# Feed-forward layers of a ten-layer fp32 network in two halves, with high and low input parts in one 512-column product

## What is computed

```python
def rmsnorm(x, g):
    return x * rsqrt(mean(x * x, -1) + eps) * g
def modulate(x, g, c_act, w, b):
    m = c_act @ w + b
    shift, scale, gate = jnp.split(m, 3, axis=-1)
    h = rmsnorm(x, g) * (1.0 + scale[:, None, :]) + shift[:, None, :]
    return h, gate[:, None, :]
def swiglu(h, w_gate, w_up, w_down):
    return (jax.nn.silu(h @ w_gate) * (h @ w_up)) @ w_down
# four times (ffn0 to ffn3):  x = x + 0.5 * g * swiglu(h, ...)
# twice (cffn0, cffn1): h = rmsnorm(x, g); a, b = split(h @ w_up);
#   x = x + (silu(causal_dwconv(a, w3, b3)) * b) @ w_down       (3 taps)
```

## Time and profile before

| | |
|---|---|
| median of 3 runs (lowest, highest) | 1868.75 us (1866.80, 1869.99) |
| span of the profiled execution, first to last instruction | 1865.1 us |
| TensorE busy, matmul / weight load | 1803.1 us / 1733.4 us, 14574 each |
| DVE / ACT / POOL busy | 1323.5 / 948.5 / 377.5 us |
| TensorE clock granted, mean | 0.994 of full |
| read from HBM | 368.89 MB, 198 GB/s over the span |

### The profile page before, as it was taken

One profiled execution on the slowest core, in us unless ns is written; L12 is line 12 of the kernel. 1 busy time (PEld: TensorE's weight loads), 2 busy tenths in 40 slices (PEclk: granted clock), 3 DMA queues, 4 the chain that ended last, 5 costly groups with the idle time before them and its releaser, 6 DMA issues.

```text
span 1865.1 us, 36260 instructions
## 1 busy us (share of the span) xinstructions
PE 1803.1 (97%) x14574; PEld 1733.4 (93%) x14574; DVE 1323.5 (71%) x1824; ACT 948.5 (51%) x1357; POOL 377.5 (20%) x371
## 2 busy tenths in 40 slices
PE   3999999999999999999999999999999999999998
PEld 2999989979999999999889999988999989689998
DVE  6677877888767576768876555897666767866665
ACT  3554555474645465446465445316544533764453
POOL 1222200051222122211143221002222200431221
PEclk9999999999999999999999999999999999999999
DMA  9877835745577647675924554313555533134551
GB/s 376 319 274 279 324 113 181 277 151 226 184 290 264 256 179 293 253 279 177 372 92 161 188 191 180 142 62 114 177 183 180 180 143 133 41 109 167 191 187 67
DMA packets 51059, 371.10 MB, mean 199 GB/s; under 512 B 5664, under 2 KB 5664, under 8 KB 6048
## 3 DMA queue, kind: packets, MB, share of 16 engines
q1 hardware_dynamic: 41760, 302.85, 44.4%
q0 software_dynamic: 9216, 67.11, 9.2%
HBM read 368.89 MB, written 1.05 MB: 198 GB/s over the span
## 4 chain that ended last, share of the span: by engine, by line
PE 83%; DVE 10%; ACT 4%; issue 1%; DMA 1%; POOL 0%; POOLq 0%; SPq 0%; DVEq 0%; ACTq 0%
PE gu L721 39%; PE acc L729 8%; PE acc L728 8%; PE acc L730 8%; DVE arena L2424 3%; PE gu L1054 2%; PE gu L1193 2%; PE gu L728 2%; PE gu L730 2%; PE gu L729 2%; DVE w_lo L1876 2%; DMA mring<-in_mods 1%; DVE mring L1891 1%; DVE arena L2166 1%; PE acc L1264 1%
## 5 line engine op out<-in xcount | busy, mean ns | idle before, releaser
L1876 DVE TENSOR_TENSOR w_lo<-ring,w_hi 128x2048 fp32r<-128x2048 f32 x265 | 613.7, 2319 | 271.6 <-ACT w_hi L1442 271.5
L1442 ACT ACTIVATE w_hi<-ring 128x2048 fp32r<-128x2048 f32 x265 | 504.9, 1907 | 74.6 <-PE acc L730 49.3
L721 PE MATMUL gu<-Hs_hi,w_hi 128*128 128x258 f32 (+1 forms) x2112 | 427.8, 284 | 2.5 <-DVE Hs_lo L1940 1.3
L721 PE MATMUL gu<-Hs_lo,w_hi 128*128 128x258 f32 (+1 forms) x2112 | 423.1, 282 | 0.0
L721 PE MATMUL gu<-Hs_hi,w_lo 128*128 128x258 f32 (+1 forms) x2112 | 422.5, 281 | 0.0
L651 POOL TENSOR_TENSOR arena<-arena,rstd 128x512 f32<-128x512 f32 x132 | 201.0, 1523 | 831.1 <-ACT arena L1456 778.4
L721 PEld LDWEIGHTS gu<-Hs_hi,w_hi 128*128 128x128 f32 x2112 | 325.7, 189 | 4.8 <-issue 1.8
L721 PEld LDWEIGHTS gu<-Hs_hi,w_lo 128*128 128x128 f32 x2112 | 325.8, 189 | 0.0
L721 PEld LDWEIGHTS gu<-Hs_lo,w_hi 128*128 128x128 f32 x2112 | 325.4, 189 | 0.0
L729 PE MATMUL acc<-hid_lo,w_hi 128*128 128x256 f32 x1056 | 297.8, 282 | 0.0
L728 PE MATMUL acc<-hid_hi,w_hi 128*128 128x256 f32 x1056 | 296.4, 281 | 1.2 <-DVE hid_lo L2095 1.2
(11 more groups left out here) (413 smaller groups left out, 2841.5 us busy)
## 6 DMA issues: line engine op xcount, KB each, us to landing
ring<-in_weights SPq DMA_DIRECT2D x276, 1024.0 KB, 4.8
mring<-in_mods POOLq DMA_DIRECT2D x64, 1024.0 KB, 6.1
mring<-in_mods SPq DMA_DIRECT2D x8, 1024.0 KB, 7.5
con<-in_constants SPq DMA_DIRECT2D x1, 1408.0 KB, 12.1
X<-in_x SPq DMA_DIRECT2D x1, 1024.0 KB, 7.2
out<-X SPq DMA_DIRECT2D x1, 1024.0 KB, 3.9
cact<-in_c SPq DMA_DIRECT2D x1, 512.0 KB, 3.3
vec<-in_vectors SPq DMA_DIRECT2D x1, 498.0 KB, 4.1
```

What stands on the lines that cost most here:

```text
L721: ins = mm(dst, part, x_lo if i == 1 else x_hi, start=start and i == 0, stop=stop and i == 2, skip_group_check=True)
L1442: act.activation(w_hi[buffer_of(n0, s)][:, :], ring[:, n % RING, :], ACT.Copy).then_inc(hi_ready, 1)
L1876: dve.tensor_tensor(w_lo[b][:, :], ring[:, n % RING, :], w_hi[b][:, :].bitcast(F32), ALU.subtract).then_inc(split_ready, 1)
```

## The change

What it does, on each engine:

- **The order of a layer.** 12 gate/up slots, 6 down slots (hidden tiles 0 to 11), 10 gate/up slots, 5 down slots (hidden tiles 12 to 21). Down goes output tile by output tile, over all hidden tiles of the half, with the last two hidden tiles of outputs 0 to 2 put behind their others; each output tile has a bank of `acc` for itself (m % 4), and each half is added to X by itself (`partial`). `clear` is gone. All is written out, without hardware loops. The weights are packed on the host in the new order; slots and bytes are as many as before.
- **Three bare hidden tiles.** Hidden tiles 0, 1, 2 are computed from the bare input as before (`bare_gate_up`, 258 columns in the layers with a shift; tile 2 in two banks of `acc`). Meanwhile the input is normalised in place, tile by tile: DVE multiplies X by gain and `row` (`scaled`), ACT adds the shift and rounds to `Hs_hi` (`normal`), DVE subtracts (`normal_low`). From hidden tile 3 on the input is final, and no shift columns and no scaling by POOL are needed.
- **The 512-column product.** For hidden tiles 3 to 21 and for all of down a product is two matmuls (`paired`): `w_hi` by the high and the low input side by side (512 columns, read from two places, `twin`) into the two halves of a bank, and `w_lo` by the high input (256 columns) onto the first half. The two halves are added behind PSUM: gate/up by ACT, which copies the second halves out (`low_half`), and DVE, which adds the first halves (`add`); down by two DVE operations into X.
- **Work that moves.** The multiplication by up and the low part of the hidden tile go from DVE to POOL (`mul`, `low`); the first of the three taps goes to ACT (`tap`). DVE's `low` for a slot now comes two slots ahead instead of three, behind `add`.
- The tiles of the next layer are entered one by one as the second half finishes them. The modulation loads keep their order by number; their folds lie at the slots of `FOLD_SLOTS`.

The diff, cut to its core:

```diff
+HALF_F0, HALF_N = (0, 12), (12, 10)
+DOWN_SLOT, DOWN_N = (12, 28), (6, 5)
+def down_tiles(half):
+    n = HALF_N[half]
+    order = [(m, f) for m in range(3) for f in range(n - 2)]
+    order += [(m, f) for m in range(3) for f in (n - 2, n - 1)]
+    return order + [(m, f) for m in range(3, KD) for f in range(n)]
...
# TensorE
+            def paired(bank, w, cols, x_both, x_hi, start, stop):
+                mm(bank.rearrange("p (a t) -> p a t", a=2), w_hi[w][:, cols], x_both, start=start, stop=False,
+                   skip_group_check=True)
+                return mm(bank[:, 0:L], w_lo[w][:, cols], x_hi, start=False, stop=stop, skip_group_check=True)
+                def gate_up(f):
+                    s = gu_slot(f)
+                    pe.wait_ge(split_ready, s0 + s + 1)
+                    pe.wait_ge(pair_free, f0 + (f - 2 if f < BARE_F + 2 else f - 1))
+                    bank = bank_of(f)
+                    for k in range(KD):
+                        if f == BARE_F:
+                            state["nh"] += 1
+                            pe.wait_ge(nh_ready, state["nh"])
+                        for e, cols in enumerate(columns(k)):
+                            ins = paired(bank[:, e, :], buffer_of(n0, s), cols, hs_twin(k), Hs_hi[:, k, 0:L],
+                                         start=(k == 0), stop=(k == KD - 1))
-                def clear():
-                    for b in range(4):
-                        mm(acc[:, b, :], zeros[:, 0:P], zeros[:, 0:1].to_broadcast([P, 512]), start=True, stop=True,
-                           skip_group_check=True)
...
-                gate_up(1)
-                clear()
-                with pe.Fori(0, ROUNDS) as it:
-                    for s in (2, 5):
-                        gate_up(s, it)
-                        gate_up(s + 1, it)
-                        down(s + 2, (s - 2) // 3, it)
-                down(FSLOTS - 1, PAIRS - 1, last=True)
+                bare_gate_up(1)
+                bare_gate_up(2)
+                for f in range(BARE_F, HALF_F0[1]):
+                    gate_up(f)
+                down(0)
+                for f in range(HALF_F0[1], NF):
+                    gate_up(f)
+                down(1)
...
# ScalarE, the start of a layer with a shift
+                high(n0, 2)
+                root(D, acc[:, 3, :])
+                evacuate(0)
+                high(n0, 3)
+                act.wait_ge(spread_ready, state["spread"])
+                act.activation(row, acc[:, 3, L:2 * L], ACT.Copy).then_inc(row_ready, 1)
+                silu(0)
+                evacuate(1)
+                for m in range(3):
+                    normal(m)
+                high(n0, 4)
+                for m in range(3, KD):
+                    normal(m)
+                silu(1)
+                high(n0, 5)
+                evacuate(2)
+                high_hidden(0)
+                high_hidden(1)
+                silu(2)
+                high_hidden(2)
...
+                    low_half(f)
+                        high_hidden(f - 1)
+                        high(n0, s + 3)
+                        silu(f)
# VectorE
+                low(n0, 3)
+                dve.wait_ge(row_ready, i + 1)
+                scaled(0)
+                scaled(1)
+                for m in range(KD):
+                    normal_low(m)
+                    if m + 2 < KD:
+                        scaled(m + 2)
+                low(n0, 4)
...
+                        add(f)
+                        low(n0, s + 2)
...
+                    fold_at(s)
+            def partial(m, how):
+                bank = acc[:, m % 4, :]
+                    link(dve.scalar_tensor_tensor(out=X[:, m, :], in0=bank[:, L:2 * L], scalar=gate[:, how, m:m + 1],
+                                                  in1=X[:, m, :], op0=ALU.mult, op1=ALU.add))
+                    return dve.scalar_tensor_tensor(out=X[:, m, :], in0=bank[:, 0:L], scalar=gate[:, how, m:m + 1],
+                                                    in1=X[:, m, :], op0=ALU.mult, op1=ALU.add)
# GpSimd, the start of a layer
+                scale(0)
+                scale(1)
+                mul(0)
+                mul(1)
+                scale(2)
+                low(0)
+                low(1)
+                mul(2)
+                low(2)
```

More of the change, by code:

```diff
@@ L655, in ffn @@
                         done += 1
-                assert done == len(folded)
+                    mul(f)
+                    low(f)
+                assert done == len(folds)
             ffn("ffn0")
@@ L678, in _ @@
         def _(pe):
-            state = dict(h=0, free=0, sq=0, misc=0, split=0, hid=0, rcp=0, presum=0, conv=0)
+            state = dict(h=0, nh=0, free=0, sq=0, misc=0, split=0, hid=0, rcp=0, presum=0, conv=0)
             mm = pe.matmul
@@ L1386, in norm @@
             def norm(scale, shift=None, mod=False, dest=H, parts=False, hi=None):
-                for m in range(KD):
-                    state["x"] += 1
-                    act.wait_ge(x_ready, state["x"])
-                    act.activation(H[:, m, :], X[:, m, :], ACT.Square).then_inc(sq_ready, 1)
                 root(D)
@@ new lines, in ffn @@
+                if conv:
+                    tap(0)
+                    tap(1)
+                    high(n0, 5)
+                    silu(0)
+                    silu(1)
+                    evacuate(2)
+                    high_hidden(0)
+                    high_hidden(1)
+                    low_half(3)
+                    tap(2)
+                    high(n0, 6)
+                    tap(3)
+                    silu(2)
+                    high_hidden(2)
+                else:
+                    silu(1)
+                    high(n0, 5)
+                    evacuate(2)
+                    high_hidden(0)
+                    high_hidden(1)
+                    silu(2)
+                    high_hidden(2)
@@ new lines, in ffn @@
+                for s in range(DOWN_SLOT[1], FSLOTS):
+                    if s == DOWN_SLOT[1]:
+                        if conv:
+                            silu(NF - 1)
+                        high_hidden(NF - 1)
+                    if s + 3 < FSLOTS:
+                        high(n0, s + 3)
+                    elif then is not None and s + 3 < FSLOTS + 2:
+                        if s + 3 == FSLOTS and extra is not None:
+                            extra()
+                        high(then, s + 3 - FSLOTS)
+                    if tiles is not None:
+                        for m in finished_in(1, s):
+                            tiles(m)
@@ L2112, in ffn @@
                 state["hid"] += NF
-                state["split"] += FSLOTS
-                update_ffn(n0, how, then, square=i != 1, enter=enter, scale=scale, parts=parts)
             def misc_wait():
```

671 lines of the change are left out of this document (401 added, 270 removed).

## The result

| | before | after |
|---|---|---|
| median of 5 runs each, in turns (lowest, highest) | 1866.80 us (1865.88, 1869.99) | 1874.58 us (1872.01, 1876.22) |
| ratio, 95% interval | | 1.0041 (1.0028 to 1.0053) |
| span of the profiled execution | 1865.1 us | 1873.6 us |

A forecast was written before the change was run, and what follows sets the result against it. TensorE's matmuls were taken as the bound, busy 1803.1 of 1865.1 us. 1865.1 - 31.1 (products) - 5.3 (`clear`) - 2 (layer ends) + 14 (layer starts) = 1840.7 us span, so 1844 median; range 1809 to 1869.

The forecast's parts named there:

- Products: TensorE's 2880 feed-forward products in two matmuls instead of three: 344.9 ns each, 10.8 less, 31.1 us less in all.
- W = 227: Assumed nanoseconds of one 512-column rounded matmul on TensorE, within bounds of 216 and 235.8.
- W = 230 to 233: The 512-column matmul's nanoseconds if the cost beyond its columns is a growing share; a fixed sum gave 225.
- The row behind it: Trace row of a rounded 384-column matmul behind a bf16 one: 170 to 180 ns, 10 to 20 beyond its columns.
- `clear`: 24 zeroing matmuls of 220 ns on TensorE's path go: 5.3 us less.
- Work behind PSUM: DVE, ACT and POOL work in steady state fits the 5.52 us slot, DVE 5.44 at most: costed at nothing.
- The start of a layer: New TensorE waits for low weights: 2.5 us in each of four layers, 2.0 in two conv layers; 14 us more.
- Ends of layers: Output tiles finish one by one, so the gaps in nsa's first slot go: 2 us less.
- The first: Rival: the 512-column matmul's fixed cost goes altogether, W = 216, 31.7 us below the forecast: 1812; chance 0.22.
- the two on the slower side: Rivals: cost by the column plus a jump, 1877, chance 0.13; a wait in each gate/up slot, 1901, chance 0.07.
- The second: Rival: 512 columns pay by the column plus a jump between places, W = 238.4: 1877; chance 0.13, split included.
- over 353: Sign of being wrong: nanoseconds from a 512-column matmul's start over the next two products' pair, 345 expected; under 335 also counted.

The follow-up runs named there:

- runs 2 and 3: The changed kernel with the 512 columns read from other places (1873.69 us); the changed kernel with 384 instead of 512 columns in most products (1776.91 us).
- run 9: Three 256-column matmuls a product instead of two, on the changed kernel with layer-start work and folds reordered (1859.66 us): 1863.12 us, ratio 0.9988 to the kernel before.
- runs 4 to 8: The changed kernel with small operations, folds or diagonals around layer starts reordered, each built on an earlier one: 1866.22, 1862.60, 1859.66, 1858.47 and 1857.40 us.
- run 1: The changed kernel with each 512-column matmul sent as two of 256, three matmuls a product: 1881.93 us, ratio 1.0079 to the kernel before.
- run 10: DVE's low weights written in four operations of 512 columns, on the changed kernel with layer-start work and folds reordered (1859.66 us): 1881.18 us, ratio 1.0080.

## Why the prediction was wrong

- **Products, the failing step.** The term "W = 227" was mis-sized: it measured 234 ns, 1 to 2.5 ns short of twice a matmul of 256. That is just above the "W = 230 to 233" that the forecast took for a growing share. The row behind it gave 10 to 20 ns beyond the columns at 384, and with 11.2 at 256 the upper end leads to 242 at 512, so the row allowed 234 from the start. I took a value between a fixed and a growing surcharge when the row could not tell them apart; runs 2 and 3 show it grows, 0.452 ns a column. Measured 9.6 us less in place of 31.1. Of the 9.6, gate/up's 256 columns in place of 258 bring 3.3 (1216 products x 3 x 2 columns x 0.45 ns), a term that the forecast carried without naming it, and the form itself some 3.5 (run 9). The rest lies in down, whose slots are shorter with three matmuls too; the change also took the hardware loop away there, and no run tested that by itself. 21.5 us of the error lie in this step. The Trainium skill ("TensorE: Matmul & The Clock Gate", "Back-to-back issue gap") gives N/2.4 + 2.5 ns, and calls it the gap of an isolated matmul, which the prediction did not say. By the trace the fixed part is about right and the column too cheap for the rounded format (234 ns measured, 215.8 by the rule); the trace decides against it.
- **`clear`**: right, 5.3 us; no L774 is left.
- **Work behind PSUM**: no wait showed in the steady state, as forecast, but the 5.44 us at most for DVE were 6.08 (POOL beside it stretches the folds from 1.22 to 1.6 or 1.75 us). Had the product been as short as forecast, ffn0's folded slots would have eaten part of the gain.
- **The start of a layer, the second failing step.** The place, the chain and the engine were right. The size was not: 25.3 us in place of 14, and 26.7 with the 0.7 at the end of each conv layer that the forecast had as fitting. "2.5 us" at slot 5 was 3.25 in ffn0 to ffn2 and 4.0 in ffn3; slot 4, given "0.1 us of room", came 0.3 to 1.0 late; conv layers lost 2.5 in place of 2.0 at slots 5 and 6; 3.2 us were the slow clock behind the gap in ffn2 and ffn3. The walk used each operation's duration alone and let POOL and DVE run side by side, where each held the other up (POOL's L733 2.71 us for 0.61, DVE's `scaled` 1.42 for 0.48).
- **Ends of layers**: nsa's gaps are gone, as forecast (from the end of cffn0 to cffn1 180.9 us in place of 183.3).
- **The rivals.** The first, on the faster side, needed 216 ns and falls with 234: the surcharge grows with the columns, so it is not a load of weights that only a short matmul leaves open. Neither of the two on the slower side happened as written. The second put its threshold at W = 236.8, with waits of 14 us; with the waits as they are it lies 12.7 / 2880 = 4.4 ns lower, at 232.4, and 234 is above it. The rivals varied one term at a time, and the loss came from two moderate misses together: 21.5 + 12.7 = 34.2 us, against 32.9 between the forecast span and the measured one. Either alone would have left the time inside the range (1865.5 and 1856.7). Of the forecast's own signs, "over 353" for the pair's distance came at the edge (353.8 in gate/up, 349.4 in down), the waits of the starts stayed under 30, and DVE's 84% in ffn0 was right.
- **From span to median**: 3.65 us was too much. Where a run stands beside its own span, they differ by 1.9 us (1875.52 and 1873.6).

The waits belong to the order of the instructions and not to the idea: runs 4 to 8 take away 17 us of the changed kernel's time by order alone. The idea as such is worth little even so: with the waits gone, run 9 prices the two-matmul product at 3.5 us. More comes from `clear` (5.3) and the shift columns (3.3), and neither needs the two-matmul product. The conv layers' 2.5 us at slots 5 and 6 stayed; that their chain through ScalarE's taps makes them was not shown, and a version that shortens it wasn't tried.

## What to carry to other kernels

Before merging two matmuls into a wider one, find out whether their overhead is per instruction or per column: one row of another width settles it, and a row that allows both answers must be priced at both ends. Where several engines hand small work on in a chain, walk the chain with the durations that two engines have side by side, and after moving one step look one slot further: the wait is likely to come back there.

## What the runs showed of the hardware that I had not expected

- A rounded fp32 matmul in a stream costs 118.2 ns for 256 columns, 176.8 for 384, 234 for 512, at the full clock: about 0.452 ns a column, 2.5 fixed, from one run or from two places alike.
- POOL operations of 0.61 to 0.74 us take up to 2.8 us beside DVE's subtraction of two SBUF operands (2.28 us), ending 0.5 to 0.6 us behind it; and DVE's operations are stretched by POOL's (a `scaled` of 0.48 us took 1.42 in ffn2 beside a POOL operation that ended 0.3 us ahead of it). Splitting the DVE operation (run 10) turned one long wait into many short ones, at a loss.
- Behind gaps of 3.3 to 4.0 us TensorE ran some 3 us at the lower clock level in two layers of four, and not in the others; with three matmuls a product and the same gaps (run 1) it did so in all four.
